# Two norms taken from one set of rows, and a merge ahead of the low halves of the weights, in a two-block transformer kernel

## What is computed

```
x = x + merged @ w_out                      # first block: attention and pool, gated
z = square(relu(rmsnorm(x, norm_mlp_g) @ w_up))
x = x + z @ w_down
x = rmsnorm(x, final_norm_g)                # last norm of the first block
h = rms_norm(x, ln_mix_g)                   # first norm of the second block
u = h @ w_in_2 ...                          # its projections
k, v = rms_norm(mem, ln_mem_g) @ w_xkv      # needs only the memory
rmsnorm(x, g) = x * rsqrt(mean(x * x) + 1e-6) * g
```

## Time and profile before

| what | value |
|---|---|
| median of 3 runs | 904.09 us (902.77 to 907.32) |
| the profiled execution | 902.93 us |
| its span in the trace | 901.1 us |
| mean granted clock of TensorE in it | 0.977 |
| PE busy | 838.7 us, 93% |
| DVE busy | 598.3 us, 66% |
| ACT busy | 450.9 us, 50% |

### The profile page before, as it was taken

One profiled execution on the slowest core, in us unless ns is written; L12 is line 12 of the kernel. 1 busy time (PEld: TensorE's weight loads), 2 busy tenths in 40 slices (PEclk: granted clock), 3 DMA queues, 4 the chain that ended last, 5 costly groups with the idle time before them and its releaser, 6 DMA issues.

```text
span 901.1 us, 13061 instructions
## 1 busy us (share of the span) xinstructions
PE 838.7 (93%) x5359; PEld 745.7 (83%) x5359; DVE 598.3 (66%) x938; ACT 450.9 (50%) x793; POOL 94.9 (11%) x105
## 2 busy tenths in 40 slices
PE   5998999979999999978999899999986999999897
PEld 4876887759999888867988688999775899999785
DVE  5777667766666755455568686656766589998543
ACT  5655556525555544254375446652565455555332
POOL 6000000000000000000400000000000245555000
PEclk9999999989999999989999999999999899999999
DMA  9744645345555555263855333335432355555451
GB/s 273 246 145 136 200 133 170 117 145 183 188 186 183 189 190 187 99 229 78 246 152 188 94 94 94 117 118 184 159 125 92 96 188 186 180 179 177 168 187 47
DMA packets 84939, 142.94 MB, mean 159 GB/s; under 512 B 4962, under 2 KB 43136, under 8 KB 84880
## 3 DMA queue, kind: packets, MB, share of 16 engines
q1 hardware_dynamic: 82704, 137.11, 46.3%
q0 software_dynamic: 2016, 4.93, 2.0%
q10 hardware_dynamic: 160, 0.07, 0.0%
HBM read 140.53 MB, written 1.05 MB: 157 GB/s over the span
## 4 chain that ended last, share of the span: by engine, by line
PE 74%; DVE 13%; ACT 7%; DMA 3%; issue 2%; POOL 0%; POOLq 0%; DVEq 0%; ACTq 0%
PE PS L1077 72%; DVE low_r L2007 6%; PE PS L1086 3%; ACT high L1602 2%; ACT WK_f L1599 2%; DMA low_f<-in_w_up_dram 1%; DVE AR_f L2015 1%; ACT XN L1599 1%; DVE WK_f L2015 1%; DMA low_f<-in_w_in_dram 1%; DMA low_f<-in_w_xq_dram 1%; DVE AR_f L2007 1%; DVE WK_f L2011 1%; DVE HTl_f L2007 1%; ACT HTh L1602 0%
## 5 line engine op out<-in xcount | busy, mean ns | idle before, releaser
L2007 DVE TENSOR_TENSOR low_r<-low_f,high 128x1024 fp32r<-128x1024 f32 x254 | 321.4, 1312 | 87.7 <-ACT high L1602 87.5
L1602 ACT ACTIVATE high<-low_f 128x1024 fp32r<-128x1024 f32 (+1 forms) x262 | 256.1, 1029 | 82.0 <-DMA low_f<-in_w_down_dram 40.2
L1077 PE MATMUL PS<-HTh,high 128*128 128x256 f32 x888 | 254.7, 287 | 2.0 <-DVE HTl_r L2007 2.0
L1077 PE MATMUL PS<-HTl_r,high 128*128 128x256 f32 x888 | 252.2, 284 | 0.0
L1077 PE MATMUL PS<-HTh,low_r 128*128 128x256 f32 x856 | 243.1, 284 | 0.0
L1077 PE MATMUL PS<-high,AR_r 128*128 128x512 f32 (+1 forms) x656 | 197.1, 383 | 10.7 <-DVE AR_r L2007 5.9
L1077 PEld LDWEIGHTS PS<-HTh,high 128*128 128x128 f32 x888 | 170.9, 192 | 4.0 <-issue 2.8
L1077 PEld LDWEIGHTS PS<-HTl_r,high 128*128 128x128 f32 x888 | 170.8, 192 | 0.1
L1077 PEld LDWEIGHTS PS<-HTh,low_r 128*128 128x128 f32 x856 | 164.6, 192 | 0.0
L1077 PEld LDWEIGHTS PS<-high,AR_r 128*128 128x128 f32 (+1 forms) x656 | 119.6, 185 | 35.8 <-issue 6.9
L1077 PE MATMUL PS<-low_r,AR_r 128*128 128x512 f32 (+1 forms) x328 | 123.9, 381 | 0.0
(11 more groups left out here) (165 smaller groups left out, 859.4 us busy)
## 6 DMA issues: line engine op xcount, KB each, us to landing
low_f<-in_w_in_dram SPq DMA_DIRECT2D x41, 1024.0 KB, 5.2
low_f<-in_w_up_dram SPq DMA_DIRECT2D x38, 1024.0 KB, 5.1
low_f<-in_w_down_dram SPq DMA_DIRECT2D x27, 1024.0 KB, 4.9
low_f<-in_w_out_dram SPq DMA_DIRECT2D x8, 1024.0 KB, 5.0
low_f<-in_w_xkv_dram SPq DMA_DIRECT2D x4, 1024.0 KB, 5.6
low_f<-in_w_branch_gla_dram SPq DMA_DIRECT2D x2, 1024.0 KB, 5.0
low_f<-in_w_branch_nsa_dram SPq DMA_DIRECT2D x2, 1024.0 KB, 5.0
low_f<-in_w_xq_dram SPq DMA_DIRECT2D x2, 1024.0 KB, 5.3
```

Of the source, the lines that this page charges most:

```text
L1077: return nc.tensor.matmul(o, l, r, start=start, stop=stop, skip_group_check=True)
L1602: return nc.scalar.activation(o, i, ACT.Copy, bias=0.0, scale=1.0)
L2007: return nc.vector.tensor_tensor(o, a, b, op)
```

## The change

It has two parts.

**Part one.** In stage one the first three pieces of `merge(1)` (the inverse and root, and the products and sums of both row blocks) are put ahead of the first tile, and both turns after the third tile. `raw_norm` stays where it was.

**Part two.** Both norms are taken from the rows before the first of them is applied. With S the sum of x*x, S_g that of (x*g)*(x*g), and a = S + 1024 eps: the last norm of the first block has the factor r1 = sqrt(1024/a), and since its result is r1*x*g, the next norm times the first one is x*g * sqrt(1024 / (S_g + eps*a)). A new `two_norms(i)` has `two_sums` (ACT: squares of X; DVE: `XN = X * grow`), `two_gained` (ACT: squares of XN; DVE: four instructions of a column or two that end in one inverse for both factors), `two_roots` (ACT: one root for both) with `scaled` (DVE: `XN` times its factor, in place), then both transposed groups at once with `HTl_f` twice and `HTl_r` twice, and, in its last piece, `final1`, which multiplies the rows X by r1 and the gain. The squares' own output goes to the rows of the memory (`AR_f`), which have been read by then. TWO_NORMS is the same string; the last piece of both norms, `final1`, lies behind all of PE's work in the stage.

```
-OUT_RATIO = 1.0
...
     def two_norms(self, i):
         self.step("warm")
-        self.step("rms", i=i, src="x2")
+        self.step("two_sums", i=i)
+        yield
+        self.step("two_gained", i=i)
+        yield
+        self.step("two_roots", i=i)
+        self.step("scaled", stage=2, i=i)
+        yield
+        for g in range(2):
+            self.turn_ht(2, i, g, "XN", self.small)
+        for g in range(2):
+            self.turn_lo(2, i, g)
         yield
         self.step("final1", i=i)
-        self.step("rms", i=i, src="xf")
         yield
-        self.step("scaled", stage=2, i=i)
-        for g in range(2):
-            self.turn_ht(2, i, g, "XN", self.small)
-            self.turn_lo(2, i, g)
-            yield
...
-        self.weave(self.chain(self.given("out", self.tiles("out", 8)), self.quad("up", 0)),
-                   self.chain(self.merge(1, self.small), self.raw_norm(1, "out")), OUT_RATIO)
+        last = self.merge(1, self.small)
+        for _ in range(3):
+            next(last)
+        out = self.given("out", self.tiles("out", 8))
+        for _ in range(3):
+            next(out)
+        self.all(last)
+        self.weave(self.chain(out, self.quad("up", 0)), self.raw_norm(1, "out"), 1.0)
...
+            def two_sums(s):
+                i = s["i"]
+                c = 40 + 8 * i
+                act.wait_ge(s_mt, 4)
+                for j in range(2):
+                    h = slice(512 * j, 512 * j + 512)
+                    act.wait_ge(*U["down", i, j].read)
+                    fsum(MEM[:, i, h], X[:, i, h], ACT.Square, st[:, c + j:c + j + 1]).then_inc(*own.up())
+
+            def two_gained(s):
+                i = s["i"]
+                c = 42 + 8 * i
+                for j in range(2):
+                    h = slice(512 * j, 512 * j + 512)
+                    act.wait_ge(s_txg, 2 * i + j + 1)
+                    act.wait_ge(*own.now())
+                    m = fsum(MEM[:, i, h], XN[:, i, h], ACT.Square, st[:, c + j:c + j + 1])
+                m.then_inc(s_tsq, 1)
+
+            def two_roots(s):
+                i = s["i"]
+                r = st[:, 44 + 8 * i:46 + 8 * i]
+                act.wait_ge(s_tinv, i + 1)
+                fn(r, r, ACT.Sqrt, scale=1024.0).then_inc(s_trt, 1)
...
+            def two_sums(s):
+                i = s["i"]
+                dve.wait_ge(s_grow, 16)
+                dve.wait_ge(s_msum, 2)
+                for j in range(2):
+                    h = slice(512 * j, 512 * j + 512)
+                    dve.wait_ge(*U["down", i, j].read)
+                    tt(XN[:, i, h], X[:, i, h], grow[:, h], ALU.mult).then_inc(s_txg, 1)
+
+            def two_gained(s):
+                i = s["i"]
+                w = st[:, 40 + 8 * i:48 + 8 * i]
+                dve.wait_ge(s_tsq, i + 1)
+                ts(w[:, 5:6], w[:, 0:1], w[:, 1:2], 1024.0 * EPS, ALU.add, ALU.add)
+                tt(w[:, 4:5], w[:, 2:3], w[:, 3:4], ALU.add).then_inc(*own.up())
+                dve.wait_ge(*own.now())
+                stt(w[:, 4:5], w[:, 5:6], EPS, w[:, 4:5], ALU.mult, ALU.add).then_inc(*own.up())
+                dve.wait_ge(*own.now())
+                nc.vector.reciprocal(w[:, 4:6], w[:, 4:6]).then_inc(s_tinv, 1)
...
+                if s["stage"] == 2:
+                    dve.wait_ge(s_trt, i + 1)
+                    ts(XN[:, i, :], XN[:, i, :], st[:, 44 + 8 * i:45 + 8 * i], None, ALU.mult).then_inc(s_xn, 1)
+                    return
...
-                dve.wait_ge(s_rs, RMS["x2", i])
+                dve.wait_ge(s_trt, i + 1)
...
-                    stt(X[:, i, h], X[:, i, h], st[:, 4 * i + 3:4 * i + 4], grow[:, h], ALU.mult,
+                    stt(X[:, i, h], X[:, i, h], st[:, 45 + 8 * i:46 + 8 * i], grow[:, h], ALU.mult,
```

More of the change, by code:

```diff
@@ L981, in two_blocks @@
         s_rsq, s_rinv, s_xf = sem("raw_sum"), sem("raw_inv"), sem("x_final1")
+        s_txg, s_tsq, s_tinv, s_trt = sem("gained"), sem("two_sums"), sem("two_inv"), sem("two_root")
         s_rope, s_angle, s_cs, s_lsum, s_lexp, s_nlam = (
@@ L1016, in two_blocks @@
         SCALED = {(s["stage"], s["i"]): s.k + 1 for s in S.steps if s.name == "scaled"}
-        SCALED_OF = {0: "x", 2: "xf", 4: "x4"}
+        SCALED_OF = {0: "x", 4: "x4"}
         RESIDUAL = {1: "out", 3: "out2"}
@@ L1638, in rms @@
                         act.wait_ge(s_x[i], 16)
[L1639 to L1643, removed]
                     else:
@@ L1994, in scalar_program @@
                        "attn_v": attn_v, "pool_d": pool_d, "merge_s": merge_s, "merge_t": merge_t,
-                       "raw_squares": raw_squares, "mem_norm": mem_norm, "mem_t": mem_t, "kv": kv, "small": small,
+                       "raw_squares": raw_squares, "two_sums": two_sums, "two_gained": two_gained,
+                       "two_roots": two_roots, "mem_norm": mem_norm, "mem_t": mem_t, "kv": kv, "small": small,
                        "cmp_z": cmp_z, "cmp_g": cmp_g, "gat": gat, "al": al, "gla_a": gla_a, "gla_e": gla_e, "gla_k": gla_k,
@@ L2680, in vector_program @@
             nc.vector.memset(eps[:, 0:1], 1.0).then_inc(s_eps, 1)
-            run_steps({"split_lo": split_lo, "gain0": gain0, "rms": rms, "scaled": scaled, "turn_ht": turn_ht, "turn_lo": turn_lo, "wide": wide,
+            run_steps({"split_lo": split_lo, "gain0": gain0, "rms": rms, "scaled": scaled, "two_sums": two_sums, "two_gained": two_gained, "turn_ht": turn_ht, "turn_lo": turn_lo, "wide": wide,
                        "tall": tall, "quad": quad, "columns": columns, "angles": angles, "lam": lam,
```

## The result

| what | before | after |
|---|---|---|
| median of 3 runs | 904.09 us | 893.14 us (891.68 to 893.22) |
| the profiled execution | 902.93 us | 893.22 us |
| its span | 901.1 us | 891.4 us |
| mean granted clock | 0.977 | 0.981 |

The account below looks back on a forecast made before the run. PE, busy 93% of the span, was taken as the bound, so only its waits and half clock could be won. Part one 3.9 plus part two 7.9 gave 11.8 us: 904.09 - 11.8 = 892.3 us, range 888.3 to 896.8.

Parts of the forecast that it names:

- I take 2.3 us of it on the unit: Stage one: POOL's 1 MB, travelling beside w_up's second unit, makes that unit land 2.3 us later.
- the bound of 2.6 us: Stage one: the most that the memory's 1 MB could delay w_up's second unit, 2.6 us at 410 GB/s.
- the lower bound of 2.6 us: Part one's least gain, 2.6 us, if the unit took the whole transfer delay and half clock lasted through the tile.
- rival 1: Stage one: the memory's transfer delays nothing, so part one gives 6.6 us and the time is 889.6 us; chance 0.23.
- (a): Stage two: kx0's low half loses the inverse ahead of it, so PE's 2.29 us pause goes; alone worth nothing.
- (b): Stage two: DVE's inverse waits for both kinds of squares; first transposes come at 401.95, against 402.15, the same.
- (c): Stage two: from 401.95 PE's work takes 15.3 us plus 1.4 us for half clock behind a 2.6 us pause, ending 418.65.
- the upper bound, 9.3 us: Part two's largest gain, 9.3 us, if no half clock follows the pause ahead of the first transposes.
- (d): End of stage two: `final1`, 2.7 us, stands ahead of the first kv unit's low halves, with 3.8 us of cover.
- Rival 2: Stage two: part two gives half, if squares or turns are 4 us late behind DVE's one wait: 896.3 us; chance 0.17.
- rival 4: Stage one: slower, as w_out's last low halves wait for the merge's links beyond 4.9 us of cover: 909 us; chance 0.02.
- Rival 3: Further on: a POOL-timed or late transfer takes the gain back, less than 4.5 us left, 900 to 904 us; chance 0.06.

Follow-up runs that it names:

- e1: The kernel before with part one alone: 900.91 us, ratio 0.9973 to the kernel before.
- e6: The changed kernel itself, run once more: 892.63 us, ratio 0.9869 to the kernel before.
- e3: The changed kernel with one more wait on POOL, so the memory's 1 MB is asked for after ACT's last squares of stage one: 888.49 us, ratio 0.9823.
- e5: The changed kernel with the late memory and another TWO_NORMS string, row block 0's transposes behind kx1's second half: 889.05 us, ratio 0.9844.
- e8: The changed kernel with only the second 0.5 MB of the memory asked for late, behind ACT's last squares of stage one: 889.88 us, ratio 0.9847.
- e9: The changed kernel with the late memory, the same program as e3, run once more: 888.04 us, ratio 0.9831 to the kernel before.
- e2: The changed kernel with stage one's order as before, so part two alone: 895.24 us, ratio 0.9901 to the kernel before.
- e7: The kernel before with one wait less on POOL, so the memory's 1 MB is asked for earlier: 903.95 us, ratio 1.0001.
- e10: The changed kernel with the late memory and the other TWO_NORMS string, the same program as e5, once more: 891.02 us, ratio 0.9869.

## Why the prediction was right, and where it was off

**What bounded the kernel.** Right. Both stages gave what PE waited for, 2.2 and 9.3 us. Outside them the trace entered stage one 0.6 us late and lost 1.2 us behind 451 us, so the span gained 9.7.

**Part one, 3.9 us predicted, 2.2 us measured** (32.68 - 30.48; e1 2.34, e6 2.30). The links came at 177.45 and ended at 181.09, 3.64 us as before; both turns' low halves ended at 186.83, ahead of the fourth tile's end; both old pauses went. The sum of tile (0,0) was late by 0.39 us (0.8 predicted). The step that was mis-sized is "I take 2.3 us of it on the unit": it was 3.6 us (9.04 - 5.40), outside even the bound of 2.6 us that I had set by the bytes at 410 GB/s, and the gain lies under the lower bound of 2.6 us. The bound counted POOL's bytes alone and not SP's third unit, which was under way as well, nor the 1.2 us that e3 shows even without the memory; which of the two made the rest is open. e3's stage one is 3.1 us shorter than the change's, e5's, where the unit landed in 5.30 us, is 4.4 us shorter. e5 is what rival 1 described, and its 32.68 - 26.09 = 6.6 us is the bound of 6.6 us that the prediction gave for it. The rest of the sum held: from the end of the sum for (1,0), 200.76, to w_up's first matmul 5.24 us, predicted 203.7 - 198.5 = 5.2, with half clock behind the pause (0.50 from 202 to 204); without it, in e3, 4.6 us.

**Part two, 7.9 us predicted, 9.3 us measured** (37.17 - 27.85; e6 9.5). (a) kx0 at once: right. (b) the first transposes 12.55 us behind the down tiles: 12.25. Pauses of 1.4 and 2.6 us: 1.22 and 2.14. (c) is the step that was mis-sized: "the clock will stand at 0.50 for some 2.9 us" behind that pause, 1.4 us. It stayed at 1.00 in after, e3, e6, e8 and e9, and fell in e2, whose 29.22 us are the 29.3 us of the prediction. So the upper bound, 9.3 us "without half clock", is the common case. The prediction took from the Trainium skill (TensorE: Matmul & The Clock Gate, Part 1: The HAM clock gate), which says that the monitor doesn't start anew with the kernel, that one length of pause may or may not be followed by half clock; the six traces agree with it, five to one. (d) `final1`: right, from 400.07 on PE's next pause of over 0.2 us is the one that ends at 451.42.

**Sum.** One part was 1.7 us too high and the other 1.4 us too low, so the forecast of 11.8 us looks better (12.0 by the ratio, 11.0 by the medians) than its terms were: that it came so close is luck. Rival 2 (half of part two) and rival 4 (slower) saw nothing of theirs happen. Rival 3 named a transfer that lands late further on, and no such wait came. Some 1.2 us were given back by the clock instead, near 451 us in one trace and near 536 us in the other; whether the kernel before loses as much on average is not shown.

**Three figures of the prediction don't follow from their terms.** The lower bound of part one, 2.6 us: 0.3 us more on the unit and 1.4 us more at half clock leave 3.9 - 1.7 = 2.2 us. The 889.9 us without half clock in (c): 1.4 us off the 892.3 give 890.9. The range's lower end of 888.3 us: that is both upper bounds in full (904.09 - 6.6 - 9.3 = 888.2), not half way.

**The best version** is e3: 888.49 us, and 888.04 in e9, 1.8% and 1.7% under the kernel before, and 0.4% under the change. Stage one accounts for 3.1 us of that step.

## What to carry to other kernels

When a step is moved ahead, look at what other queues ask for on its signal: here the gain of the reordering was more than halved (2.2 us of stage one against 5.3 in e3) because POOL's 1 MB left 0.24 us ahead of the one unit that PE needed next, and one wait that sends it later, when nobody is in a hurry, gave back 3.3 to 4.0 us. Price such a meeting by all the bytes under way until the unit is in, the next unit's too, and not by a share; and try a delay, since in e7 the memory asked for 2.3 us behind the unit cost nothing. Two traces of one kernel are needed before a microsecond far from the edit is put down to it.

## What the hardware showed that was not expected

- Two transfers of 1 MB from different queues, asked for within 0.3 us, landed 9.0 us (SP's) and 8.8 us (POOL's) after their requests, where in the kernel before, apart from each other, they took 5.4 and 5.6 us (in e2, which has the same order there, POOL's took 7.0). That is 1 us more than the second one's 2.6 us at 410 GB/s. For one microsecond of that time (189 to 190) the engines were busy by a share of 0.78 and moved only 162 GB/s. What they did is open, but the meeting isn't needed for it: in e3, without the memory, 187 to 188 shows a share of 0.87 and 135 GB/s.
- Pauses of the same place and length were followed by full clock or by half: 1.89 us (e3: none, after: 6 us), 2.14 us (five traces without, one with). In both traces of one program (e5 and e10) half clock stood behind 2.1 us and 1.64 us, while the pause of 1.65 us at the same place in e3, e6, e9 and after, and that of 2.55 us in e8, had full clock behind it: no length divides them. Whether a shift of the whole program by a microsecond would lift them was not tried, so what decides it stays open.
- The unit that landed 6.5 us after its request in e3 and e9, and 5.3 us in e5 and e10, with nothing else asked for: in e3 the windows of a microsecond show 403, 174 and 8 GB/s from 189 to 192, and a share of 0.05 in the last of them. The last bytes were late, the cause is not known.
